# Twenty of the first projection's units computed in ten pairs by Strassen's algorithm

## The reference

```python
def short_conv_fourier_mixer(h, w_in, conv_w, w_out):
    proj = h @ w_in                      # h: rms_norm(x), [1024 tokens, 1024]; w_in: [1024, 3072]
    a_x, a_b, a_c, a_z, b_u, b_z = jnp.split(proj, [...])          # six parts, each 512 wide
    y_a = a_b * centred_depthwise_conv(a_c * a_x, conv_w) * jax.nn.silu(a_z)
    f = jnp.fft.fft2(u, axes=(1, 3), norm="ortho").real            # u: b_u in four groups of 128
    y_b = f.reshape(bsz, s, B_WIDTH) * jax.nn.silu(b_z)
    return jnp.concatenate([y_a, y_b], axis=-1) @ w_out
```

## Time and profile before

| | us |
|---|---|
| median of three runs | 1753.91 (1752.42 to 1754.14) |
| the profiled execution, device time | 1752.93 |
| its span, first to last instruction | 1751.1 |
| PE busy in the span | 1710.2 |
| POOL busy in the span | 452.9 |

### The profile page before, as it was taken

How to read it: one execution, slowest core, us unless ns; L and a number is a source line. 1 busy time by engine, 2 the same in 40 slices (tenths; PEclk the granted TensorE clock), 3 DMA queues, 4 the chain that set the end, 5 groups by cost and what they waited for, 6 DMA issues and landing times.

```text
span 1751.1 us, 21292 instructions
## 1 busy us (share of the span) xinstructions
PE 1710.2 (98%) x8348; PEld 1416.2 (81%) x8348; DVE 1051.2 (60%) x1281; ACT 661.6 (38%) x845; POOL 452.9 (26%) x288
## 2 busy tenths in 40 slices
PE   7999999999999999999999999999999999999997
PEld 6888888888788888887888877788888788778885
DVE  7342335445677777877775799255655277887223
ACT  6110112225566655576622422110124667682002
POOL 4233233332210110101022332232333222214330
PEclk9999999999999999999999999999999999999999
DMA  5121131132101111011332211112123311336112
GB/s 213 37 72 65 57 132 37 48 136 80 37 1 37 37 37 37 1 37 37 149 123 96 97 36 49 65 38 78 62 91 126 121 49 61 121 133 241 49 36 96
DMA packets 40674, 133.70 MB, mean 76 GB/s; under 512 B 5516, under 2 KB 5900, under 8 KB 40320
## 3 DMA queue, kind: packets, MB, share of 16 engines
q1 hardware_dynamic: 40288, 131.83, 21.1%
q10 hardware_dynamic: 288, 0.52, 0.1%
HBM read 100.61 MB, written 31.59 MB: 75 GB/s over the span
## 4 chain that ended last, share of the span: by engine, by line
PE 87%; DVE 8%; ACT 3%; issue 2%; DMA 0%; SPq 0%; DVEq 0%; ACTq 0%
PE pair L836 49%; PE pair L1055 8%; PE pair L1118 5%; PE aux L1091 4%; PE pair L1104 3%; PE pair L847 2%; PE pair L1399 2%; PE aux L1270 1%; PE pair L855 1%; PE pair L911 1%; PE aux L836 1%; DVE stat_b L2183 1%; PE pair L1384 1%; PE pair L1412 1%; PE aux L1412 1%
## 5 line engine op out<-in xcount | busy, mean ns | idle before, releaser
L737 POOL CAST w_hi<-w_raw 128x1024 fp32r<-128x1024 f32 x106 | 117.6, 1109 | 1111.0 <-issue 1102.5
L836 PE MATMUL pair<-op_hi,w_hi 128*128 128x512 f32 x990 | 307.4, 392 | 0.9 <-DVE op_lo L1954 0.9
L836 PE MATMUL pair<-op_lo,w_hi 128*128 128x512 f32 x990 | 305.0, 389 | 0.0
L836 PE MATMUL pair<-op_hi,w_lo 128*128 128x512 f32 x990 | 304.9, 389 | 0.0
L739 POOL TENSOR_TENSOR w_lo<-w_raw,w_hi 128x1024 fp32r<-128x1024 f32 x106 | 271.9, 2565 | 8.5
L836 PEld LDWEIGHTS pair<-op_hi,w_hi 128*128 128x128 f32 x990 | 185.5, 188 | 41.7 <-issue 2.6
L836 PEld LDWEIGHTS pair<-op_lo,w_hi 128*128 128x128 f32 x990 | 186.0, 188 | 39.0
L836 PEld LDWEIGHTS pair<-op_hi,w_lo 128*128 128x128 f32 x990 | 185.8, 188 | 38.9
L1649 ACT ACTIVATE pt_hi<-pair 128x1024 fp32r<-128x1024 f32 x60 | 61.7, 1028 | 126.7 <-issue 84.6
L1949 DVE TENSOR_TENSOR pt_lo<-pair,pt_hi 128x1024 fp32r<-128x1024 f32 x60 | 73.5, 1225 | 52.4 <-ACT pt_hi L1649 48.9
L1055 PE MATMUL pair<-opb_hi,w_hi 128*128 128x512 f32 x256 | 101.7, 397 | 1.1 <-DVEq L86 0.6
(11 more groups left out here) (403 smaller groups left out, 3076.5 us busy)
## 6 DMA issues: line engine op xcount, KB each, us to landing
w_raw<-weight_units SPq DMA_DIRECT2D x106, 512.0 KB, 3.5
xf<-y_dram SPq DMA_DIRECT2D x12, 512.0 KB, 4.7
x_dram<-xa SPq DMA_DIRECT2D x8, 512.0 KB, 5.9
xc<-x_dram SPq DMA_DIRECT2D x8, 512.0 KB, 7.9
x_dram<-xc SPq DMA_DIRECT2D x8, 512.0 KB, 2.6
y_dram<-y_d SPq DMA_DIRECT2D x8, 512.0 KB, 2.6
mz_dram<-y_d SPq DMA_DIRECT2D x8, 512.0 KB, 2.9
bm_b<-bm_dram SPq DMA_DIRECT2D x8, 512.0 KB, 4.8
```

The lines of the kernel that those rows point to most:

```text
L737: pool.tensor_copy(w_hi[:, u % 2, :], w_raw[:, u % 3, :]).then_inc(w_hi_done, 1)
L836: mm = pe.matmul(acc[:, cols], w, x[:, kx, cols], start=(first and k == 0 and n == 0), stop=(last and k == KT - 1 and n == 2))
```

## The change

Units 0 to 3 stay as they were. Units 4 to 23 are taken in ten **pairs** q = 0 to 9. A pair's two units and the activations form a product of 2 x 2 blocks: the weights of unit e0 split into its k-tiles 0 to 3 (a) and 4 to 7 (b), those of e1 likewise, and the activations into k-tiles 0 to 3 or 4 to 7 by the left or right 512 tokens. Winograd's form of Strassen's algorithm computes the four output blocks (C11 and C12 are unit e0, left and right tokens; C21 and C22 are unit e1) with seven block products of 12 matmuls of 512 columns:

- P1 = e0a x (k 0-3, left), P2 = e0b x (k 4-7, left), P5, P6, P7, P3 and P4 with sums on one or both sides. C11 = P1 + P2; U2 = P1 + P6; C12 = U2 + P5 + P3; C22 = U2 + P7 + P5; C21 = U2 + P7 - P4, the sign taken up by the operand.
- P1, P6, P7 and P4 pile up in the same half of `pair[1]` (the half alternates with q). After P1 and after P6 the bank is copied out by ACT before PE may add the next product. P5 and P3 share a half of `pair[0]`, P2 has the other.
- PE's order is P1(q), P4(q-1), P5(q), P6(q), P2(q), P7(q), P3(q); `fft_time` stands behind P5, `fft_channels` behind P2 (for group 0 behind P3(0)).
- Sums of activations, once, at the start: `cmb_raw` and the reused halves of `xa` on DVE, hi parts on ACT (`cmb_hi`, `xa_cmb`), lo parts on DVE and, for P7, on POOL. `xa` is thereby overwritten and loaded again from `x_t` before the residual.
- Sums of weights, for each pair four on DVE (`weight_sum`, sum 0 for P5, 1 for P6, 2 for P7, 3 for P3, into three buffers `w_sum`).
- POOL splits 512-wide **blocks** instead of units, one for each product (`block`), into a ring of four places in `w_hi` and `w_lo`: a block may be made once the product four places ahead of it is done.
- The outputs: ACT copies P1, P6 and P5 (512 columns each), DVE adds `add_c11`, `add_c22`, `add_c12` and takes C21 (`take_c21`).
- `w_raw` has four buffers instead of three, and some semaphores are merged.

Pair q is of kind (q + 2) % 3: kind 2 holds a_b and a_z (q = 0: of group 0; for it b_z is unit 3), kind 0 b_u and a_x of the next group, kind 1 a_c and b_z.

```diff
+FAST = 4
+PAIRS = (EVEN_IN - FAST) // 2
+QUAD = KT // 2
+RING_STEP = 8
+AFTER_P1 = {"P1": -1, "P5": 1, "P6": 2, "P2": 3, "P7": 4, "P3": 5}
+SUM_OF = {"P5": 0, "P6": 1, "P7": 2, "P3": 3}
+def place(q, name):
+    if name == "P4":
+        return 7 * q + (7 if q < PAIRS - 1 else 6)
+    return max(7 * q + AFTER_P1[name], 0)
...
+            def block(q, name):
+                at, u = place(q, name), FAST + 2 * q
+                half, cols = ring(at) // 2, slice(ring(at) % 2 * HALF, (ring(at) % 2 + 1) * HALF)
+                hi, lo = w_hi[:, half, cols], w_lo[:, half, cols]
+                if name in SUM_OF:
+                    pool.wait_ge(sum_made, 4 * q + SUM_OF[name] + 1)
+                    src = w_sum[:, SUM_OF[name] % 3, :]
+                elif name == "P4":
+                    pool.wait_ge(w_loaded[(u + 1) % RAW], 16 * ((u + 1) // RAW + 1))
+                    src = w_raw[:, (u + 1) % RAW, HALF:S]
+                else:
+                    pool.wait_ge(w_loaded[u % RAW], 16 * (u // RAW + 1))
+                    src = w_raw[:, u % RAW, 0:HALF] if name == "P1" else w_raw[:, u % RAW, HALF:S]
+                if at < 4:
+                    pool.wait_ge(unit_done, FAST - 1 + half)
+                else:
+                    pool.wait_ge(product_done, at - 1 if at - RING_STEP in (0, 1) else at - 3)
+                pool.tensor_copy(hi, src).then_inc(w_hi_done, 1)
+                pool.wait_ge(w_hi_done, FAST + at + 1)
+                pool.tensor_tensor(lo, src, hi, ALU.subtract).then_inc(block_made, 1)
+            for u in range(2, FAST):
+                split(u)
+            block(0, "P1")
+            pool.wait_ge(copied, QUAD + 2)
+            pool.tensor_tensor(cmb_lo[:, 1], cmb_raw[:, 1], cmb_hi[:, 1], ALU.subtract).then_inc(cmb_low_p7, 1)
+            for q in range(PAIRS):
+                if q >= 1:
+                    block(q, "P1")
+                    block(q - 1, "P4")
+                block(q, "P5")
+                block(q, "P6")
+                block(q, "P2")
+                block(q, "P7")
+                block(q, "P3")
+            block(PAIRS - 1, "P4")
+            for u in range(BASE[1], BASE[5]):
                 split(u)
...
+            def product(q, name):
+                at = place(q, name)
+                half, col0 = ring(at) // 2, ring(at) % 2 * HALF
+                hi, lo = operands[name]
+                first = name in ("P1", "P2", "P5")
+                pe.wait_ge(block_made, at + 1)
+                if name == "P1":
+                    pe.wait_ge(pair_free[1], FAST // 2 + max(q - 1, 0))
+                elif name in ("P5", "P2"):
+                    pe.wait_ge(pair_free[0], FAST // 2 + q)
+                elif name == "P6":
+                    pe.wait_ge(copied, copy_at(q, "P1"))
+                elif name == "P7":
+                    pe.wait_ge(copied, copy_at(q, "P6"))
+                elif name == "P3":
+                    pe.wait_ge(copied, copy_at(q, "P5"))
+                else:
+                    pe.wait_ge(c22_added, q + 1)
+                if q == 0 and name == "P7":
+                    pe.wait_ge(cmb_low_p7, 1)
+                elif q == 0 and name in ("P5", "P6", "P4"):
+                    pe.wait_ge(cmb_low, ("P5", "P6", "P4").index(name) + 1)
+                for k in range(QUAD):
+                    cols = slice(col0 + k * P, col0 + (k + 1) * P)
+                    for n, (w, x) in enumerate(((w_hi, hi), (w_hi, lo), (w_lo, hi))):
+                        mm = pe.matmul(accumulator(q, name), w[:, half, cols], x[:, k, :],
+                                       start=(first and k == 0 and n == 0),
+                                       stop=(k == QUAD - 1 and n == 2), skip_group_check=(not first))
+                mm.then_inc(product_done, 1)
+            for u in range(2, FAST):
+                unit(u, u, op_hi, op_lo, "even")
+            for q in range(PAIRS):
+                j, turn_of = mixer_of(q)
+                product(q, "P1")
+                if q >= 1:
+                    product(q - 1, "P4")
+                product(q, "P5")
+                if q == 1:
+                    fft_time(0)
+                elif q >= 3 and turn_of == 2:
+                    fft_time(j)
+                product(q, "P6")
+                product(q, "P2")
+                if turn_of == 1:
+                    fft_channels(j)
+                product(q, "P7")
+                product(q, "P3")
+                if q == 0:
+                    fft_channels(0)
+            product(PAIRS - 1, "P4")
...
+            act.wait_ge(op_ready, QUAD)
+            for k in range(QUAD):
+                link(act.activation(xa[:, k, HALF:S], xa[:, k, HALF:S], ACT.Copy, scale=col("norm_even", k)), copied)
+            wait_job(act, 0)
+            link(act.activation(bu_row, pair[0][:, :], ACT.Copy), bu_ready)
+            signal(pair_free[0])
+            wait_job(act, 1)
+            link(act.activation(ax_sb[:, :], pair[1][:, :], ACT.Copy), ax_ready)
+            signal(pair_free[1])
+            norm_rstd(1, aux[:, 0:S], rstd_a)
+            act.wait_ge(cmb_summed, 1)
+            link(act.activation(cmb_hi[:, 0], cmb_raw[:, 0], ACT.Copy, scale=-1.0), copied)
...
+            copy_p1(0)
+            copy_p5(0)
+            copy_u2(0)
+            fourier_gate(0)
+            spectrum(0)
+            for q in range(1, PAIRS):
+                j, kind = mixer_of(q)
+                copy_p1(q)
+                if kind == 0:
+                    conv_gate(j - 1)
+                    copy_u2(q)
+                    copy_p5(q)
+                    continue
+                if kind == 2:
+                    fourier_gate(j)
+                copy_p5(q)
+                copy_u2(q)
+                if kind == 1:
+                    spectrum(j)
+            for k in range(THROUGH["y1"]):
+                y_hi("y1", k, y1_in[k], op_hi)
+            conv_gate(AB - 1)
...
+            def gained_sum(out, k, cols, other, op):
+                link(dve.scalar_tensor_tensor(out=out, in0=xa[:, k, cols], scalar=col("norm_even", k), in1=other,
+                                              op0=ALU.mult, op1=op))
+            left, right = slice(0, HALF), slice(HALF, S)
+            for k in range(QUAD):
+                dve.wait_ge(copied, k + 1)
+                gained_sum(cmb_raw[:, 0, k, :], k, left, xa[:, k, right], ALU.subtract)
+            signal(cmb_summed)
+            for k in range(QUAD):
+                gained_sum(cmb_raw[:, 1, k, :], QUAD + k, right, xa[:, k, right], ALU.subtract)
+            signal(cmb_summed)
+            for k in range(QUAD):
+                gained_sum(xa[:, k, right], QUAD + k, right, cmb_raw[:, 0, k, :], ALU.add)
+            signal(cmb_summed)
+            for k in range(QUAD):
+                gained_sum(xa[:, QUAD + k, left], QUAD + k, left, xa[:, k, right], ALU.subtract)
+            signal(cmb_summed)
+            dve.wait_ge(copied, QUAD + 1)
+            link(dve.scalar_tensor_tensor(out=cmb_lo[:, 0], in0=cmb_raw[:, 0], scalar=-1.0, in1=cmb_hi[:, 0],
+                                          op0=ALU.mult, op1=ALU.subtract), cmb_low)
+            def weight_sum(q, n):
+                u = FAST + 2 * q
+                e0, e1 = w_raw[:, u % RAW, :], w_raw[:, (u + 1) % RAW, :]
+                if n == 0:
+                    dve.wait_ge(w_loaded[u % RAW], 16 * (u // RAW + 1))
+                    dve.wait_ge(w_loaded[(u + 1) % RAW], 16 * ((u + 1) // RAW + 1))
+                    if q >= 1:
+                        dve.wait_ge(block_made, place(q - 1, "P3") + 1)
+                    link(dve.tensor_tensor(w_sum[:, 0, :], e1[:, 0:HALF], e1[:, HALF:S], ALU.add), sum_made)
+                elif n == 1:
+                    link(dve.tensor_tensor(w_sum[:, 1, :], w_sum[:, 0, :], e0[:, 0:HALF], ALU.subtract), sum_made)
+                elif n == 2:
+                    link(dve.tensor_tensor(w_sum[:, 2, :], e0[:, 0:HALF], e1[:, 0:HALF], ALU.subtract), sum_made)
+                else:
+                    dve.wait_ge(block_made, place(q, "P5") + 1)
+                    link(dve.tensor_tensor(w_sum[:, 0, :], e0[:, HALF:S], w_sum[:, 1, :], ALU.subtract), sum_made)
...
+            def take_c21(q):
+                dst = second_row[mixer_of(q)[1]]
+                dve.wait_ge(product_done, place(q, "P4") + 1)
+                link(dve.tensor_tensor(dst[:, left], accumulator(q, "P4"), rstd_a[:, left], ALU.mult))
+                signal(pair_free[1])
+                link(dve.tensor_tensor(dst[:, right], dst[:, right], rstd_a[:, right], ALU.mult))
+            dve.wait_ge(ax_ready, 1)
+            by_token(ax_sb[:, :], ax_sb[:, :])
+            for n in range(3):
+                weight_sum(0, n)
+            wait_job(dve, 2)
+            link(dve.tensor_tensor(u_pad[:, 1:S + 1], pair[0][:, :], ax_sb[:, :], ALU.mult))
+            free(2)
+            dve.wait_ge(copied, QUAD + 3)
```

(45 more changed lines are left out.)

338 lines of the change are left out of this document (195 added, 143 removed).

## The result

The changed kernel takes **1777.47 us** (median of four runs, 1777.2 to 1777.81); the kernel before took 1754.03 us beside it. The ratio is 1.0138, interval 1.0123 to 1.0152: 1.4% slower, 17.5 us above the forecast and above its range. The profiled execution took 1777.4 us, its span 1775.0.

A forecast was written before the change was run, and what follows sets the result against it. PE's matmuls were taken to bound the first projection. -27.2 (matmuls) + 15.3 (start) + 9.6 (rounds) + 8.4 (end) = +6.1 us on 1752.9 gave 1759.0, as a median 1760 us; range 1740 to 1772.

The forecast's parts named there:

- Matmuls, -27.2: First projection: 960 matmuls become 840, 120 fewer at 0.2268 us each, 27.2 us less PE work.
- The exclusion of DVE and POOL: DVE instructions reading two SBUF operands and POOL's splits never overlap; each waits for the whole of the other, taking turns.
- The faster rival: Collisions cost less: 1745 us with half of each wait, 1734 with none; chance 0.30.
- The start, +15.3: Up to the first channel transform, PE waits for POOL's blocks and DVE's folding: 15.3 us together, 0.6 if nothing collided.
- the terms at nothing: Costed at zero: ACT's copies, the reload of x, the fourth w_raw buffer and the rest of the kernel.
- The rounds, +9.6: Three rounds of three pairs, counted from T, P3(q)'s end: PE waits 2.2 us for folding, 1.0 for ACT's copy; 9.6 us.
- The end, +8.4: After the last pair, first_pair waits 8.4 us for ACT's hi part of tile 7; 6.6 without collisions.
- The clock rival, +2.4 at most: Two waits of about 5 us or more each followed by some 6 slow matmuls: 2.4 us, 1762; chance 0.15.
- The self-feeding rival: Late foldings make DVE miss the next pair's adds, P5 waits for pair_free[0]: 11 us more, 1771; chance 0.12.
- The sum: Whole kernel: -27.2 + 15.3 + 9.6 + 8.4 = +6.1 us on the profiled execution's 1752.9.

The follow-up runs named there:

- the own buffer: Changed kernel with pair 0's first output row in y_a[:, 0] instead of fold, ACT's copy of P1(0) no longer awaiting parts_ready: 1771.48 us.
- the narrow splits: Changed kernel with POOL's casts and subtractions of blocks from the second pair on 32 columns wide, not 512: 1762.85 us.
- the new order: Changed kernel with, in the last pair, low parts 0 to 3 ahead of C22 and C12 on DVE, C21 ahead of the Fourier output: 1773.09 us.
- the late transform: On the three edits, PE's first channel transform two products later, behind P4(0), and its time transform behind P6(1): 1749.6 us.
- the three edits: Changed kernel with pair 0's copies kept out of fold, DVE's order changed in the rounds, and DVE's order changed in the last pair: 1747.09 us.
- the reordered start: On the three edits, DVE's fourth weight sum and folding ahead of the last 2048-wide low part, mixer 0's convolution behind C12(0): 1743.88 us.

## Why the prediction was wrong, point by point

- **Matmuls, -27.2**: right. 8228 of them, 0.227 us apart wherever the clock is full.
- **The exclusion of DVE and POOL**: right, in rate and in most times. The forecast's chain has the sums done at 55.0 (measured 55.0), P5's low part 57.4 (57.5), block P5 62.3 (62.35), P6's operand 65.2 (65.05), block P6 66.3 (66.2), P2 69.6 (69.4), P7 73.4 (73.15), P3 79.2 (79.96). `parts_ready` came at 84.8 and not at 87.8 in the changed kernel, since POOL had nothing to do from 80 us on while PE stood, and at 87.4 with the own buffer. The Trainium skill, "SBUF — State Buffer", section "Who interferes with whom", has the same rule, and the narrow splits bear it out: the weight sums beside them take 0.69 us. The faster rival, half the collisions, did not occur (its 3 us for the rounds are not half of 9.6 either, and the forecast gives no working for them).
- **The start, +15.3: the step that failed.** The forecast had "5.9 before `fft_channels(0)`, since P3 ends at 81.9", so it took the transform as the only one to wait for `parts_ready`; and among the terms at nothing it had "ACT's copies (covered by two products each". The change has the line in which ACT's `copy_p1` waits for `parts_ready` too (shown with the result), and `product` the line in which P6 waits for that copy. So the copy of P1(0) was not covered by two products: it came 23.4 us after P1(0) had ended (84.79 against 61.4). PE stopped 19.9 us at P6(0) with four products still to do, and the transform began at 98.95 and not at 87.8. With an own buffer it begins at 87.43: the time was right for the kernel that the forecast had in mind, and the single waits in part (1.3 before P1(0), which it did not have, then 1.2, 0.6, 0.2, 0.7, 3.8 and 1.9 against its 2.8, 1.3, 0.6, 1.1, 3.0 and 5.9; the slow P3(0) fills a part of the last).
- **The rounds, +9.6**: 11.4 of waits, each forecast in its place, and 2.0 slow. Right in mechanism, short by a fifth in size. One sum in it does not come out: a folding that ends at T + 8.4 alone and meets eleven turns of 0.8 us ends at T + 17.2, not 15.8. In the trace it ends near T + 16.
- **The end, +8.4**: 7.7 of waits where they were forecast, for `op_hi`; with the slow matmuls 11.4. The forecast said that without collisions 6.6 would be left, since the queue's order alone makes tile 7 late; the narrow splits do not test this (those of units 24 and 25 stay 1024 wide), the new order does: more than half of the price was the order.
- **The clock rival, +2.4 at most**: the mechanism was there, the price was 8.2. It was asked of waits of "about 5 us or more" and of 6 matmuls each. The first wait of 2.6 us was followed by five slow pairs of matmuls, that of 19.9 us by 12 slow matmuls, those of `first_pair` by 16. The Trainium skill, "TensorE: Matmul & The Clock Gate", section "HAM oscillation", describes kernels whose clock falls in the wait of each step; this trace now shows such a fall (0.50 at 85.4 to 89 us), though not in each wait, where the trace of before could show none.
- The self-feeding rival did not occur: the only waits for `pair_free` in the stretch are unit 2's 0.3 us at 35 us, which the forecast had at 0.6, and P1(0)'s 1.3 us, for ACT's copy of unit 3. No P5 waits for `pair_free[0]`.
- **The sum.** The forecast had +6.1 and the span shows +23.9, 17.8 more: 11.1 from the start (2.5 of it slow matmuls), 3.8 from the rounds, 3.0 from the end, and 1.1 that the counting of the waits leaves out, less 1.2 behind the projection.

## What to carry to other kernels

When an accumulator has to be copied out before the next product may be added, the copy's *destination* is part of PE's critical path: write down for each copy what its destination still holds and who reads it, and look for a queue entry ahead of the copy that waits for a third engine. Three times here (the `fold` buffer, the late transform, the convolution moved at the start) that decided more than the price of any instruction. A gap in PE can cost more than its length: look for slow matmuls behind every wait (in the first projection of these runs' traces behind some of 1.9 to 2.8 us and each of 3.2 us or more, behind none of 1.6 us or less, unless it came within a few us of a long one). And where matmuls are traded for vector sums, order the vector queue by what PE waits for: the same arithmetic cost 1.4% here or won 0.65%, by the order of DVE's queue and one buffer. The profile's releaser is a guess where an instruction waits for several things: at 85.48 us it named none, at 104.61 us the wrong one, and both times the copy's own row in ACT's timeline told it.

## What the runs showed of the hardware that was not expected

- The clock falls behind waits of 2.6 us, but not behind each: of the three in the changed kernel's profiled execution one was followed by 1.8 us of slow matmuls and two by 0.1; with the own buffer alone all three were (1.8, 3.2, 1.5), and so was its first transform behind a wait of 1.9 us (1.8), but not that of the three edits behind 1.8 us (0.1). The runs of the kernel with the own buffer alone spread over 7 us and those of the changed one over 0.6; that the clock makes the difference is argued from one trace of each, not shown.
- DVE's TENSOR_SCALAR on one SBUF operand takes turns with POOL as well. The convolution's first step (1024 columns) takes 0.75 us with narrow splits beside it, and with whole ones 0.98 and 1.65, each time ending 0.55 us behind POOL's instruction. The row of the reordered start:

```profile
91.08 1.65 DVE L2321 TENSOR_SCALAR ax_sb<-u_pad,par 128x1024 f32<-128x1024 f32 x1
```

- DVE's sums with an operand in PSUM (C11, C12, C22) take 0.69 us throughout, whatever POOL does.
